# The mean of the heads' squares from unsplit squares in full-precision matmuls

## The chip, the cores and the metric

The kernel runs on one core of a Trainium2 chip. The metric is the device time of one execution in microseconds (us), the median of several runs. The engines are named as the profile names them: PE is TensorE (PEld its weight loads), DVE is VectorE, ACT is ScalarE, POOL is GpSimd, SP is the queue that issues the DMAs.

## What is computed

One layer of a hybrid decoder, for a prompt of 2048 tokens and a sample group of 8 x 4 tokens with the same weights. The change touches one term: the RMS norm of each head's output of the gated linear attention.

```
def _rmsnorm(x, g):
    xf = x.astype(jnp.float32)
    y = xf * lax.rsqrt(jnp.mean(xf * xf, axis=-1, keepdims=True) + EPS)
    return (y * g.astype(jnp.float32)).astype(x.dtype)
...
    h = _rmsnorm(x, lw['g_mix_pre'])
    proj = h @ lw['w_in']
    q, k, v, r, glr, u, vs = jnp.split(proj, SPLIT_POINTS, axis=-1)
...
    o, S_new = _gla(qh, kh, vh, gh, S0.astype(jnp.float32))
    o = _rmsnorm(o, lw['g_gla_out']).reshape(n, l, GLA_WIDTH).astype(x.dtype) * jax.nn.silu(r)
...
    mix = jnp.concatenate([o, s_out], axis=-1) @ lw['w_out']
    x = x + _rmsnorm(mix, lw['g_mix_post'])
```

There are 4 heads of 128 values each; the mean of the squares goes over a head's 128 values. After the mixer come a gated feed-forward part with a causal convolution and a gated per-layer embedding.

## The kernel before

It runs in five stages one after the other: the input projection, the mixer (`phase_mix`), the up projection with the convolution, the down projection, and the embedding. Large products are made in a rounded 32-bit type (F32R): each operand is split into a rounded copy and the rest that the rounding left, and three products (copy by copy, copy by rest, rest by copy) are summed.

The mixer walks over 16 tiles of 128 tokens in one hand-written order per engine, unrolled, as a loop of passes t = 0 to 19. Pass t works on several tiles at once: it makes scores, state and outputs of tile t (`turn_keys`, `make_scores`, `mix_positions`, `make_kv`, `within_chunk`, `from_state`), prepares the gates of tile t+1 (`gate_logits`, `soft_logs`, `exps`, `v_norm`), finishes the heads of tile t-1, and projects tile t-2 with the output weights (`project`, 48 matmuls of 512 columns in four groups). Tile 16 is the sample group, whose mixer work is done in passes 0 and 1. Every engine runs its own queue in order; semaphores join them. Each `within_chunk` (lines 809 to 819) of pass t overwrites the banks `o_acc`, so TensorE waits there for `gla_outs`, which VectorE raises in `finish_gla` of tile t-1 (line 1343).

The mean of a tile's squares takes these steps:
- ScalarE, `head_squares` (lines 992 to 999): the head outputs lie in two PSUM banks, `o_acc[0]` and `o_acc[1]`, 256 columns each. It squares each bank into `square` (line 997) and, from the bank again, into the rounded tile `square_h` (line 999). Behind it in ScalarE's queue come `copy_keys` (line 1006) and `soft_logs` (lines 1016 to 1023).
- GpSimd, `split_squares` (line 1151): `square_l` is `square` less `square_h`, in one instruction. Ahead of it in the queue is `row_powers` (lines 75 and 77), behind it `open_mixed` (line 1185) and `v_scale`.
- TensorE, `average_squares` (line 789): `m.average`, a 128 x 128 matrix of 1/128, times `square_h` and times `square_l`, summed in the other half of the bank. Two banks and two parts make four matmuls of 256 columns per tile. They stand in the middle of `project` of tile t-2, between its first and second group.
- ScalarE, `inverse_norm` (lines 1043 and 1047): logarithm and exponential give the inverse root; then `exps` of tile t+1 (line 1035) follow in its queue.
- VectorE, `finish_gla` (lines 1343 and 1352), far down its queue: it begins each pass with `scale_rows` (line 1374), which waits for `row_powers`, and has `mask` (1310), `v_stats`, `add_bias` (1336), the decays (1265 to 1279) and `v_norm` (1300) ahead of `finish_gla`.

The sample group has a mean of its own (line 898), which already multiplies the unsplit squares by `m.average` cast to F32.

Of the kernel before, what the change touches and what calls it, by code (L numbers as in the profile page):

```python
# [4 lines left out]
F32 = mybir.dt.float32  # L5
F32R = mybir.dt.float32r
I32 = mybir.dt.int32
ALU = mybir.AluOpType
ACT = mybir.ActivationFunctionType


P = 128
# [393 lines left out]
def phase_semaphores(nc, ctx, tag):  # L406


    held = []

    def clear():
        nc.clear_and_free_semaphores(held)
        nc.all_engine_barrier()
    ctx.callback(clear)

    def sem(name):
        held.append(nc.alloc_semaphore(name=f"{tag}_{name}"))
        return held[-1]
    return sem
# [96 lines left out]
def phase_mix(nc, a, pt_scratch, v_scratch, vs_scratch, residual, store, state_out, sample_state_out, vn_out,  # L516
# [4 lines left out]
    with ctx:  # L521
        sb = lambda n, s, d=F32: ctx.enter_context(nc.sbuf_tensor(f"mix_{n}", s, d))
        sem = phase_semaphores(nc, ctx, "mix")
        two = lambda n, s, d=F32: [sb(f"{n}{i}", s, d) for i in range(2)]
        m = MixerConsts(nc, ctx)
# [9 lines left out]
        with ExitStack() as placed:  # L535
# [17 lines left out]
        scores = sb("scores", [P, 2, 2, C])  # L553
        k_tok = sb("k_tok", [P, 2, P])
        state = two("state", [P, 2, DV])
        square, square_h, square_l = sb("square", [P, 2, 2 * P]), sb("square_h", [P, 2, 2 * P], F32R), \
            sb("square_l", [P, 2, 2 * P], F32R)
        inv = sb("inv", [P, 2, 2 * P])
        mixed = two("mixed", [P, 2 * H, P])

# [3 lines left out]
        ks_acc, o_acc = [bank("ks0"), bank("ks1")], [bank("o0"), bank("o1")]  # L564
# [10 lines left out]
        stat, v_power, v_normed, v_gained = (sem(n) for n in ("stat", "v_power", "v_normed", "v_gained"))  # L575
        scored, masked, k_turned, k_copied = (sem(n) for n in ("scored", "masked", "k_turned", "k_copied"))
        kv_made, states, outputs, crossed_made = sem("kv_made"), sem("states"), sem("outputs"), sem("crossed_made")
        squared, square_split, averaged, inverse = (sem(n) for n in ("squared", "square_split", "averaged", "inverse"))
        spatials, gla_outs, biased, sgu_outs = (sem(n) for n in ("spatials", "gla_outs", "biased", "sgu_outs"))
        state_stored = sem("state_stored")  # L580
        high, split, summed = sem("high"), sem("split"), sem("summed")
# [27 lines left out]
        def mixes(t):  # L609
            return 0 <= t < NT  # L610

        def projects(o):
            return 0 <= o <= NT
# [119 lines left out]
        def _(pe):  # L733
# [49 lines left out]
                last.then_inc(spatials, 1)  # L783

            def average_squares(t):
                pe.wait_ge(square_split, t + 1)
                for f in range(2):
                    for p, part_ in enumerate((square_h, square_l)):
                        last = nc.tensor.matmul(o_acc[f][:, 2 * P:4 * P], m.average[:, :], part_[:, f, :],
                                                start=(p == 0), stop=(p == 1))  # L790
                last.then_inc(averaged, 1)

            def make_kv(t):
# [127 lines left out]
            for h in range(HS):  # L921
                last = nc.tensor.transpose(m_acc[:, h * P:(h + 1) * P], spatial_raw[:, h, :], ident[:, :])
# [7 lines left out]
            for t in range(LAST):  # L930
# [12 lines left out]
                if mixes(t - 1):  # L943
                    average_squares(t - 1)
# [33 lines left out]
        def _(act):  # L978
# [12 lines left out]
            def head_squares(t):  # L991
                act.wait_ge(outputs, t * 2 + 2)
                if t >= 1:

                    act.wait_ge(averaged, t)
                for f in range(2):
                    nc.scalar.activation(square[:, f, :], o_acc[f][:, 0:2 * P], ACT.Square).then_inc(squared, 1)
                for f in range(2):
                    nc.scalar.activation(square_h[:, f, :], o_acc[f][:, 0:2 * P], ACT.Square).then_inc(squared, 1)

            def copy_keys(t):
                act.wait_ge(k_turned, t + 1)
# [103 lines left out]
            for t in range(LAST + 1):  # L1106
                if projects(t - 3):
                    row_squares(t - 3, 1)
                if mixes(t - 1):
                    head_squares(t - 1)  # L1110
                if mixes(t):
                    copy_keys(t)
                if mixes(t + 1):
                    soft_logs(t + 1)
                if t == 0:
                    sample_keys()
                if mixes(t - 1):
                    inverse_norm(t - 1)
                if mixes(t + 1):
                    exps(t + 1)  # L1120
                if t == 1:
                    sample_squares()
                    sample_inverse()
                if t < 2:
                    for k in range(4 * t, 4 * t + 4):
                        round_w(k)
                if projects(t - 1):
                    rounds(t - 1)
                if projects(t - 2):
                    row_squares(t - 2, 0)  # L1130

        @block.gpsimd
        def _(pool):
            def row_powers(o):
                s, rows = o % 2, out_rows(o)
                pool.wait_ge(row_squared, o * 2 + 2)
                if o >= 2:

                    pool.wait_ge(finished, (o - 1) * 2)
                rstd_ops(nc, pool, rstd[rows, s:s + 1], [part[rows, s, 0:1], part[rows, s, 1:2]],  # L1140
                         mean[rows, s:s + 1], consts[rows, :], powers, o * 3)

            def add_rest(o):
                s, rows = o % 2, out_rows(o)
                pool.wait_ge(res_in[s], o // 2 * 16 + 16)
                pool.wait_ge(finished, o * 2 + 2)
                nc.gpsimd.tensor_tensor(y[s][rows, :], y[s][rows, :], res[s][rows, :], ALU.add).then_inc(added, 1)

            def split_squares(t):
                pool.wait_ge(squared, t * 4 + 4)  # L1150
                nc.gpsimd.tensor_tensor(square_l[:, :, :], square[:, :, :], square_h[:, :, :].bitcast(F32),
                                        ALU.subtract).then_inc(square_split, 1)

            def v_scale(t):
                pool.wait_ge(stat, t * 8 + 8)
                nc.gpsimd.tensor_tensor(v_var[:, :], mv[:, :, 1:2].rearrange("p h a -> p (h a)"),
                                        consts[:, 0:1].to_broadcast([P, HS]), ALU.add).then_inc(v_power, 1)
                pool.wait_ge(v_power, t * 2 + 1)
                nc.gpsimd.tensor_tensor(v_rstd[:, :], v_var[:, :], consts[:, 1:2].to_broadcast([P, HS]), ALU.pow)\
                    .then_inc(v_power, 1)  # L1160

            def make_keys(t):
                s = t % 2
                if t >= 2:

                    pool.wait_ge(outputs, t * 2 - 2)
                for i, (out_, e) in enumerate(((k_in[s], e_k), (k_end[s], e_end))):
                    pool.wait_ge(factors, t * 4 + (i + 1))
                    nc.gpsimd.tensor_tensor(out_[:, :, :], qk[s][:, 2:4, :],
                                            e[:, :].rearrange("p (q t) -> p q t", q=2), ALU.mult).then_inc(keys, 1)  # L1170

            def v_tail(t):
                s = t % 2
                pool.wait_ge(v_normed, t * 4 + 4)
                if t == 0:
                    pool.wait_ge(loaded, 64)
                nc.gpsimd.tensor_tensor(vn[s][:, :], vn[s][:, :], m.ln_gain[:, :], ALU.mult).then_inc(v_gained, 1)
                pool.wait_ge(v_gained, t * 2 + 1)
                nc.gpsimd.tensor_tensor(vn[s][:, :], vn[s][:, :], m.ln_bias[:, :], ALU.add).then_inc(v_gained, 1)

            def open_mixed(t):
                s = t % 2
                pool.wait_ge(b_in[s], t // 2 * 32 + 32)
                pool.wait_ge(biased, t + 1)
                nc.gpsimd.tensor_tensor(mixed[s][:, H:2 * H, :], mixed[s][:, H:2 * H, :], ru[s][:, H:2 * H, :],
                                        ALU.mult).then_inc(sgu_outs, 1)
# [47 lines left out]
            for t in range(LAST + 1):  # L1234
                if projects(t - 3):
                    row_powers(t - 3)
                if mixes(t - 1):
                    split_squares(t - 1)
                if mixes(t):
                    open_mixed(t)  # L1240
                if mixes(t + 1):
                    v_scale(t + 1)
                if projects(t - 3):
                    add_rest(t - 3)
                if mixes(t + 1):
                    make_keys(t + 1)
                    v_tail(t + 1)
# [1187 lines left out]
def build(nc, a, outs):  # L2435
# [15 lines left out]
    with ctx:  # L2451
# [19 lines left out]
        with nc.sbuf_tensor("xh", [P, KC, T], F32R) as xh, nc.sbuf_tensor("xl", [P, KC, T], F32R) as xl:  # L2471
            phase_in(nc, x_tiles, xh, xl, a["w_in"][0], gains[:, 0, :], pt, v_s, vs_s, ident, consts)

        x1_of = lambda t: x1[token_rows(t), :]
        ffn = ctx.enter_context(nc.sbuf_tensor("ffn_features", [P, 2 * FC, 20], F32))
        phase_mix(nc, a, pt, v_s, vs_s, x_tiles, x1_of, outs[2][0, 0], outs[3][0], outs[6][0].rearrange("b t n -> (b t) n"),
                  [a["state_ffn_conv"][0].rearrange("b c n -> (b c) n"), a["w_conv"][0], a["b_conv"]], ffn, ident, consts)

# [51 lines left out]
```

## Time and profile before

| | us |
|---|---|
| median of 3 runs | 2875.97 (2875.3 to 2876.09) |
| the profiled execution | 2875.3 |
| its span, first to last instruction | 2873.6 |
| PE busy | 2660.5 (93%) |
| PE weight loads busy | 2398.4 (83%) |
| DVE busy | 1066.8 (37%) |
| ACT busy | 881.5 (31%) |
| POOL busy | 539.1 (19%) |
| mean granted TensorE clock | 0.951 |

All times of the trace are microseconds from the span's start. The mixer takes about 550 to 1009 us of it. Matmuls are pipelined, so the duration recorded of one is longer than the time from one to the next; the latter tells the price. A granted clock of 1.00 is 2.4 GHz, one of 0.50 is 1.2 GHz.

### The profile page before, as it was taken

How to read it: one execution, taken by the hardware profiler on the slowest of the kernel's cores; microseconds unless marked ns; L12 is line 12 of the kernel's file. 1: busy time of each engine (PE TensorE's matmuls, PEld its weight loads, DVE VectorE, ACT ScalarE, POOL GpSimd, SP SyncE). 2: the span in 40 equal slices, each digit the busy share in tenths (PEclk: the TensorE clock that was granted, in tenths of full speed). 3: DMA queues.
4: the chain of work that ended last, by engine and by line, in shares of the span. 5: the costliest groups of instructions: out<-in, count | busy, mean ns of one | idle time of the engine just before them, and what ended most of it. 6: DMA issues, size and time to landing. Idle time of an engine off the chain costs nothing. (4 is left out here: it accounts for less than half of the span.)

```text
span 2873.6 us, 36961 instructions
## 1 busy us (share of the span) xinstructions
PE 2660.5 (93%) x13748; PEld 2398.4 (83%) x13748; DVE 1066.8 (37%) x1635; ACT 881.5 (31%) x1781; POOL 539.1 (19%) x642
## 2 busy tenths in 40 slices
PE   7999999658888869999999999999799999996998
PEld 5789999556666669999999999999678888885887
DVE  4200000257666264444444444444422242324332
ACT  3311111123333263333333333333321142214332
POOL 2100000135544231111111111111000013221222
PEclk9999999759888989999999999999899999998999
DMA  4212221523333141111111111112454476643221
GB/s 147 91 63 67 70 67 62 136 78 113 102 100 93 59 150 53 42 53 38 50 50 42 56 38 50 41 47 73 120 143 111 119 219 192 192 133 123 83 79 44
DMA packets 270523, 257.54 MB, mean 90 GB/s; under 512 B 15830, under 2 KB 232422, under 8 KB 270406
## 3 DMA queue, kind: packets, MB, share of 16 engines
q1 hardware_dynamic: 270444, 256.51, 28.9%
q8 instruction: 47, 0.77, 0.1%
q14 instruction: 32, 0.26, 0.0%
HBM read 179.20 MB, written 77.26 MB: 89 GB/s over the span
## 5 line engine op out<-in xcount | busy, mean ns | idle before, releaser
L1857 PE MATMUL up_acc<-xh,up_wh 128*128 128x416 f32 x1760 | 619.6, 352 | 0.0
L1857 PE MATMUL up_acc<-xl,up_wh 128*128 128x416 f32 x1760 | 616.5, 350 | 0.0
L1857 PE MATMUL up_acc<-xh,up_wl 128*128 128x416 f32 x1760 | 616.1, 350 | 0.0
L1784 DVE SCALAR_TENSOR_TENSOR up_conv<-up_up,ffn_features,up_conv 128x416 f32<-128x416 f32 (+1 forms) x440 | 284.1, 646 | 570.4 <-ACT up_conv L1701 558.2
L1857 PEld LDWEIGHTS up_acc<-xh,up_wl 128*128 128x128 f32 x1760 | 330.1, 188 | 4.2
L1857 PEld LDWEIGHTS up_acc<-xl,up_wh 128*128 128x128 f32 x1760 | 330.8, 188 | 2.8
L1857 PEld LDWEIGHTS up_acc<-xh,up_wh 128*128 128x128 f32 x1760 | 329.9, 187 | 2.9
L2161 PE MATMUL down_acc<-down_wh,down_sh 128*128 128x512 f32 x748 | 293.3, 392 | 23.6 <-DVE down_sl L2092 23.6
L1695 ACT ACTIVATE up_up<-up_acc 128x416 f32<-128x416 f32 (+1 forms) x220 | 113.2, 515 | 606.3 <-PE up_acc L1857 606.3
L2161 PE MATMUL down_acc<-down_wl,down_sh 128*128 128x512 f32 x748 | 292.6, 391 | 0.0
L2161 PE MATMUL down_acc<-down_wh,down_sl 128*128 128x512 f32 x748 | 292.3, 391 | 0.0
L2161 PEld LDWEIGHTS down_acc<-down_wh,down_sh 128*128 128x128 f32 x748 | 141.4, 189 | 53.8 <-DVE down_sl L2092 24.6
L2092 DVE TENSOR_TENSOR down_sl<-down_raw,down_sh 128x2816 fp32r<-128x2816 f32 x34 | 110.9, 3262 | 192.9 <-ACT down_sh L2048 187.7
L1631 POOL COPY tail<-up_up 128x2 f32 (+1 forms) x44 | 22.6, 515 | 821.8 <-ACT up_conv L1701 821.8
L2161 PEld LDWEIGHTS down_acc<-down_wl,down_sh 128*128 128x128 f32 x748 | 141.4, 189 | 29.5
L2161 PEld LDWEIGHTS down_acc<-down_wh,down_sl 128*128 128x128 f32 x748 | 141.4, 189 | 29.5
L232 DVE TENSOR_TENSOR in_wl<-in_raw,in_wh 128x1024 fp32r<-128x1024 f32 x19 | 32.2, 1705 | 337.2 <-ACT in_wh L280 337.2
L1701 ACT ACTIVATE up_conv<-up_acc,ffn_features 128x416 f32<-128x416 f32 x220 | 154.8, 704 | 0.0
L287 ACT ACTIVATE in_outs<-in_acc 128x416 f32<-128x416 f32 (+2 forms) x86 | 47.2, 549 | 339.4 <-PE in_acc L393 194.2
L393 PE MATMUL in_acc<-xh,in_wh 128*128 128x416 f32 x416 | 146.2, 351 | 0.0
L393 PE MATMUL in_acc<-xl,in_wh 128*128 128x416 f32 x416 | 145.7, 350 | 0.0
L393 PE MATMUL in_acc<-xh,in_wl 128*128 128x416 f32 x416 | 145.4, 350 | 0.0
(271 smaller groups left out, 4311.9 us busy)
## 6 DMA issues: line engine op xcount, KB each, us to landing
down_raw<-hidden SPq DMA_DIRECT2D x34, 1408.0 KB, 7.6
hidden<-up_conv SPq DMA_DIRECT2D x110, 208.0 KB, 1.9
up_raw<-in_w_up SPq DMA_DIRECT2D x44, 512.0 KB, 3.9
proj_features<-in_outs SPq DMA_DIRECT2D x65, 208.0 KB, 1.9
down_ahead<-in_w_down SPq DMA_DIRECT2D x40, 256.0 KB, 5.3
in_raw<-in_w_in SPq DMA_DIRECT2D x19, 512.0 KB, 4.2
ple_x<-x SPq DMA_DIRECT2D x17, 512.0 KB, 4.3
in_x<-in_x_prompt SPq DMA_DIRECT2D x16, 512.0 KB, 3.6
```

What stands on the lines that cost most here:

```text
L232: nc.vector.tensor_tensor(wl[:, slot[n]], raw(n)[:, :, :], wh[:, slot[n]].bitcast(F32), ALU.subtract).then_inc(ready, 1)
L287: nc.scalar.activation(out[bank][rows, 0:width], acc[rows, 0:width], func)\
L393: last = nc.tensor.matmul(acc[bank][:, 0:TB], w[:, s, k, :], x[:, k, b * TB:(b + 1) * TB], start=(k == 0 and p == 0), stop=(k == KC - 1 an ...
L1631: nc.gpsimd.tensor_copy(tail[:, at, 0:2].rearrange("p a c -> p (a c)"), up[NBLK - 1][:, LAST:LAST + 2])
L1695: nc.scalar.activation(up[b][:, 2:2 + prompt], a[:, 0:prompt], ACT.Copy)
L1701: nc.scalar.activation(conv[b][:, :], a[:, 0:TB], ACT.Identity, scale=taps[:, at, 2:3].rearrange("p a c -> p (a c)"), bias=bias[:, at]).th ...
L1784: last = nc.vector.scalar_tensor_tensor(out=out, in0=x(c), in1=out, scalar=taps[:, at, c:c + 1].rearrange("p a c -> p (a c)"), op0=ALU.mul ...
L1857: last = nc.tensor.matmul(acc[b][:, 0:TB], w[kind][:, k, :], x[:, k, b * TB:(b + 1) * TB], start=(k == 0 and p == 0), stop=(k == KC - 1 an ...
L2092: nc.vector.tensor_tensor(sl[s][:, :, :], raw[s][:, :, :], sh[s][:, :, :].bitcast(F32), ALU.subtract).then_inc(split, 1)
L2161: last = nc.tensor.matmul(acc[s][:, :], x[s][:, k, :], ww[:, k, :], start=(k == 0 and p == 0), stop=(k == FC - 1 and p == 2))
```

## The change

`head_squares` keeps only the two squares into `square`. The tiles `square_h` and `square_l`, the GpSimd step `split_squares` and its semaphore go. `average_squares` waits for the two squares of its tile and makes one matmul per bank, 256 columns, of `m.average` cast to F32 and `square`, both in full 32-bit precision.

```
-        square, square_h, square_l = sb("square", [P, 2, 2 * P]), sb("square_h", [P, 2, 2 * P], F32R), \
-            sb("square_l", [P, 2, 2 * P], F32R)
+        square = sb("square", [P, 2, 2 * P])
...
-        squared, square_split, averaged, inverse = (sem(n) for n in ("squared", "square_split", "averaged", "inverse"))
+        squared, averaged, inverse = sem("squared"), sem("averaged"), sem("inverse")
...
             def average_squares(t):
-                pe.wait_ge(square_split, t + 1)
+                pe.wait_ge(squared, t * 2 + 2)
                 for f in range(2):
-                    for p, part_ in enumerate((square_h, square_l)):
-                        last = nc.tensor.matmul(o_acc[f][:, 2 * P:4 * P], m.average[:, :], part_[:, f, :],
-                                                start=(p == 0), stop=(p == 1))
+                    last = nc.tensor.matmul(o_acc[f][:, 2 * P:4 * P], m.average[:, :].bitcast(F32), square[:, f, :],
+                                            start=True, stop=True)
                 last.then_inc(averaged, 1)
...
                 for f in range(2):
                     nc.scalar.activation(square[:, f, :], o_acc[f][:, 0:2 * P], ACT.Square).then_inc(squared, 1)
-                for f in range(2):
-                    nc.scalar.activation(square_h[:, f, :], o_acc[f][:, 0:2 * P], ACT.Square).then_inc(squared, 1)
...
-            def split_squares(t):
-                pool.wait_ge(squared, t * 4 + 4)
-                nc.gpsimd.tensor_tensor(square_l[:, :, :], square[:, :, :], square_h[:, :, :].bitcast(F32),
-                                        ALU.subtract).then_inc(square_split, 1)
-
...
-                if mixes(t - 1):
-                    split_squares(t - 1)
                 if mixes(t):
                     open_mixed(t)
```

## Rows read from the trace of the kernel before

**Rows 1.** Busy by window: us; PE, PEld, DVE, ACT, POOL (x instructions); clock, DMA share, GB/s.
```profile
640.00:945.00 305.00, 259.23 (x1702) 204.81 (x1698) 207.83 (x416) 107.75 (x286) 152.66 (x156) 0.86 0.33 99
945.00:1010.00 65.00, 51.95 (x248) 41.14 (x248) 14.39 (x27) 11.76 (x29) 17.92 (x20) 0.94 0.15 53
```
**Rows 2.** Waits, 640 to 945 us: total us, times, longest us.
```profile
PE mix_o_acc L816 <- DVE mix_mixed L1343: 45.5, 12, 3.8
```
**Rows 3.** Timeline of PE, pass 12: start, duration, instruction [idle before it and who ended it].
```profile
872.52 1.16 PE L781 MATMUL mix_m_acc<-mc_spatial,mix_vn 128*128 128x128 f32 x8
873.44 0.48 PE L846 MATMUL mix_out_acc<-mix_wh,mix_sh 128*128 128x512 f32 x1
...
876.28 0.28 PE L789 MATMUL mix_o_acc<-mix_square_h,mc_average 128*128 128x256 f32 x1
...
876.74 0.40 PE L846 MATMUL mix_out_acc<-mix_wh,mix_sh 128*128 128x512 f32 x1
...
879.61 0.67 PE L803 MATMUL mix_ks_acc<-mix_v,mix_k_tok 64*64 64x128 f32 x16
884.07 1.12 PE L816 MATMUL mix_o_acc<-mix_scores,mix_v 64*128 64x64 f32 x8 [3.79 <-DVE mix_mixed L1343]
```
**Rows 4.** Timeline of ACT, pass 12.
```profile
871.79 0.67 ACT L999 ACTIVATE mix_square_h<-mix_o_acc 128x256 fp32r<-128x256 f32 x2
872.32 0.41 ACT L1006 ACTIVATE mix_k_tok<-mix_zt_acc 128x256 f32<-128x256 f32 x1
...
877.81 0.63 ACT L1047 ACTIVATE mix_inv<-mix_inv 128x512 f32<-128x512 f32 x1
878.83 0.42 ACT L1035 ACTIVATE mix_e_k<-mix_from_mid 128x256 f32<-128x256 f32 x1 [0.38 <-DVE mix_to_end L1279]
```
**Rows 5.** Timeline of POOL, pass 12.
```profile
872.53 1.28 POOL L1151 TENSOR_TENSOR mix_square_l<-mix_square,mix_square_h 128x512 fp32r<-128x512 f32 x1
875.85 1.60 POOL L1185 TENSOR_TENSOR mix_mixed<-mix_mixed,mix_ru 128x512 f32<-128x512 f32 x1 [2.04 <-DVE mix_mixed L1336]
```
**Rows 6.** Timeline of DVE, pass 12 and (977.28) pass 17.
```profile
872.53 1.41 DVE L1374 SCALAR_TENSOR_TENSOR mix_y<-mix_out_acc,mix_rstd,mix_gain_rows 128x512 f32<-128x512 f32 x2 [6.41 <-POOL mix_rstd L77]
...
883.27 0.74 DVE L1343 TENSOR_TENSOR mix_mixed<-mix_o_acc,mix_inv 128x256 f32<-128x256 f32 x2
...
977.28 1.41 DVE L1374 SCALAR_TENSOR_TENSOR mix_y<-mix_out_acc,mix_rstd,mix_gain_rows 128x512 f32<-128x512 f32 x2 [4.42 <-POOL mix_rstd L77]
```
**Rows 7.** Timelines of PE and ACT, passes 1 and 2.
```profile
612.34 0.58 PE L789 MATMUL mix_o_acc<-mix_square_h,mc_average 128*128 128x256 f32 x1
...
613.60 0.84 ACT L1043 ACTIVATE mix_inv<-mix_o_acc,consts 128x256 f32<-128x256 f32 x2 [14.52 <-PE mix_o_acc L789]
...
636.70 1.11 PE L826 MATMUL mix_o_acc<-mix_q_state,mix_state 64*128 64x64 f32 x8 [2.17 <-DVE mix_state L1326]
```
**Rows 8.** Busy by window, as in rows 1, behind four of PE's stalls.
```profile
693.54:699.04 5.50, 5.50 (x25) 4.61 (x26) 4.82 (x8) 1.63 (x3) 1.95 (x2) 0.50 0.65 195
...
860.15:866.25 6.10, 6.10 (x26) 5.11 (x27) 5.29 (x9) 1.63 (x3) 1.96 (x2) 0.50 0.67 208
...
962.29:965.25 2.96, 2.96 (x7) 2.38 (x8) 0.51 (x1) 0.00 (x0) 2.67 (x2) 0.50 0.00 0
...
993.75:1004.80 11.05, 11.05 (x48) 8.90 (x48) 0.51 (x1) 0.68 (x2) 2.40 (x1) 1.00 0.12 47
```
**Rows 9.** Timeline of PE, its stalls in passes 16 and 18.
```profile
962.29 0.77 PE L846 MATMUL mix_out_acc<-mix_wh,mix_sh 128*128 128x512 f32 x1 [2.24 <-DVE mix_y L1374]
...
993.75 0.47 PE L846 MATMUL mix_out_acc<-mix_wh,mix_sh 128*128 128x512 f32 x1 [2.82 <-DVE mix_y L1374]
```
**Rows 10.** Timeline of PE, the ends of three holes.
```profile
670.91 0.66 PE L816 MATMUL mix_o_acc<-mix_scores,mix_v 64*128 64x64 f32 x8 [3.80 <-DVE mix_mixed L1343]
...
693.54 1.12 PE L816 MATMUL mix_o_acc<-mix_scores,mix_v 64*128 64x64 f32 x8 [3.79 <-DVE mix_mixed L1343]
...
860.15 1.12 PE L816 MATMUL mix_o_acc<-mix_scores,mix_v 64*128 64x64 f32 x8 [3.79 <-DVE mix_mixed L1343]
```

## What I predict

> **What bounds the kernel now.** I read the busy times by stage first, then the waits, then one pass of the mixer loop engine by engine. The change touches only the mixer. In its steady part TensorE is busy 259 of 305 us and its granted clock averages 0.86 [rows 1]: it is neither full nor always fast. The waits name one hole: before the matmuls of line 816 TensorE stands still 12 times, 45.5 us in all, until VectorE has written `mixed` at line 1343 [rows 2]. That is once in each of the passes t = 3 to 14.
>
> Pass 12 shows how the loop closes. TensorE's last work before the hole starts at 879.61; the hole, 3.79 us, ends at 884.07 [rows 3]. Line 1343 doesn't wait for the squares' mean: the inverse is complete at 877.81 + 0.63 = 878.44 [rows 4], and VectorE reaches line 1343 only at 883.27 [rows 6]. What holds VectorE back is its own queue. It opens with `scale_rows` at 872.53, which waited 6.41 us for GpSimd's reciprocal root [rows 6], which goes back over ScalarE's `row_squares` to TensorE's last projection. So the loop runs TensorE's projection, ScalarE's row squares, GpSimd's root, VectorE's queue, TensorE again. The mean of the squares is beside this loop, with 883.27 - 878.44 = 4.8 us to spare.
>
> **Removed on ScalarE: two Square activations per tile.** They stand ahead of `copy_keys` and take 871.79 to 872.32, 0.53 us [rows 4], in all 16 x 0.53 = 8.5 us. `copy_keys` and the logarithms behind it could move up by that much at most, but what they feed, the decays on VectorE, stands in VectorE's queue behind `scale_rows`, which their absence doesn't release. On the path: 0. If that cover were gone, 0.53 us in each of 14 passes, 7.5 us.
>
> **Removed on GpSimd: `split_squares`,** 1.28 us per tile, 20.5 us in all. In pass 12 GpSimd then stands idle for 2.04 us until VectorE's line 1336 [rows 5], so its queue gains nothing. The subtraction runs exactly beside the two `scale_rows` instructions, which are on the path. If it slowed them, its removal would pay. The pair takes 1.41 us beside it (872.53), and 1.41 us in pass 17, where there is no subtraction (977.28) [rows 6]. On the path: 0.
>
> **Moved wait.** `average_squares` now waits for the two squares, issued before 871.79, where it waited for GpSimd until 872.53 + 1.28 = 873.81 [rows 4, 5]. TensorE reaches it at 876.28 without idle [rows 3], so nothing is queued behind a new wait: 0.
>
> **Changed on TensorE: four rounded products of 256 columns become two full-precision ones.** The four take 876.28 to 876.74, 0.46 us, 0.115 each [rows 3]. No row shows a full-precision product of 256 columns. The nearest is line 781 at 128: its four products are eight recorded matmuls, so one product is two of them, and they take 872.52 to 873.44, again 0.115 each [rows 3]. If the moving columns set that figure, 256 of them need 0.23, and a tile's four matmuls 0.92 us, 0.46 more than now. If the weight load sets it, which is 128 columns wide in both lines, a tile needs 4 x 0.115 = 0.46 us, 0.00 more. Line 803 decides: it has 64 weight columns and 128 moving ones and runs four at once. Its 16 matmuls take 0.67 us [rows 3]; less some 0.28 for one alone, that is 0.13 us between fours, no less than line 781's. Half the weight width saved nothing, so I take 0.46. For something unseen I keep twice the price, 1.84 us (+1.38), as the upper end, and 0.00 as the lower.
>
> The Trainium skill bears on this choice: "FP8 and Floating Point Precision", section TensorE Precision Notes, says that true FP32 makes four passes through the array. That is the first of the two readings; by the weight-load reading the sum would lose this term.
>
> **Where the 0.46 us falls.** In the 12 passes with the hole it only shortens the hole, from 3.79 to 3.33 us. The inverse ends at about 878.9 instead of 878.44, and ScalarE's exponentials, which start at 878.83 now because VectorE's decays are late [rows 4], move by some 0.1; what they feed on GpSimd comes behind 2 us of other work. So 12 x 0.
>
> Four tiles have no hole behind them.
> - Tile 0 (pass 1), at 612.34. The matmul is recorded at 0.58 us against 0.28 in pass 12, so the clock is at half, and ScalarE waited for the mean 14.52 us [rows 3, 7]. From there ScalarE, VectorE's queue and the sample matmuls lead without a gap to 636.70 [rows 7]. Cost at half clock: 2 x 0.46 = 0.9 us.
> - Tile 1 (pass 2): TensorE runs through to its projection: +0.46.
> - Tiles 14 and 15 (passes 15 and 16): TensorE is continuous up to its stalls, one of them before 962.29 [rows 9]: +0.46 each.
>
> Raw delay: 0.9 + 3 x 0.46 = 2.3 us. Not all of it lasts. Behind each hole the granted clock is 0.50, the lower of its two levels, 1.2 GHz: for 5.50 us in pass 4 and for 6.10 us in pass 11 [rows 8], though the work is the same. The period grows from 22.63 us (670.91 to 693.54) to 23.92 us (860.15 to 884.07) [rows 3, 10]. I read this as a loop that settles: a pass that starts later against the clock's return spends less time at half clock and gives part of the delay back. A delay brought in by tiles 0 and 1 should have died out by pass 14, and I count it 0 (end of the range 0.9 + 0.46 = 1.4). Left are tiles 14 and 15, 0.9 us.
>
> **Forecast.** The profiled execution's span is 2873.6 us, 2875.3 with what lies around it, 0.7 below the median. Against its own time the sum is 2876.2; on the median, 2875.97 + 0.9 = **2876.9 us**. What moves this by more than its own size is the clock at the mixer's end. A stall of 2.24 us before 962.29 is followed by 2.96 us at half clock, while one of 2.82 us before 993.75 costs none [rows 8, 9]. Shifting these stalls by 0.5 to 0.9 us may swap one for the other, 2.96 / 2 = 1.5 us either way for each, and the next stage begins at a clock that has to rise too.
>
> **Rivals.**
> - *The shorter hole keeps the clock up (faster).* "TensorE: Matmul & The Clock Gate" in the Trainium skill, section Why this matters for your kernels, asks for no long idle gaps between bursts, since the clock then falls; by that rule a shorter hole may be a gain. From rows: 6.10 us at half clock on the path are worth 3.05 us, times 11 about 33 us, hence 2843 us. Against it: a stall of only 2.24 us lost the clock [rows 8, 9], and the hole stays at 3.33. For it: one of 2.82 us kept it. Chance 0.04.
> - *The removed work was on the path after all (faster).* ScalarE's 7.5 us, hence 2869.4 us with the 0.9. Against it: the readings above [rows 4 to 6]. Chance 0.03.
> - *The full-precision product costs twice my price (slower).* At +1.38 us the 12 holes of 3.79 still cover it. Tile 0 at half clock costs 2.8, tiles 1, 14 and 15 1.4 each, 7 us if nothing is given back, hence 2883 us. It decides from +1.15 a tile (5 x 1.15 = 5.75). For it: no row at 256 columns. Against it: lines 781 and 803. Chance 0.06.
> - *The product isn't made in full precision* (two rounded products): 0.23 us saved in each of two tiles, 2875.5 us. Against it: no row; it would need the cast in the diff to be without effect. Chance 0.02.
>
> **How the numbers follow.** Forecast 0.85. A measurement of this kernel can tell about 0.2%, 5.75 us, from no change. Faster 0.04 + 0.03 less what of them stays small: 0.06. Slower 0.06. Within 0.2%: 0.88. The range is the forecast with three clock swaps of 1.5 us either way, and the 1.4 us of tiles 0 and 1 on the slow side, less what is unlikely to come together: 2872 to 2881.5 us.
>
> **What would show it.** In the changed profile: no GpSimd work between the root and line 1185, and 3.3 us idle before the latter; four recorded matmuls a tile at the mean, 0.23 us apart at full clock; the stall before line 816 still 12 times, near 3.3 us, with late periods of 23.9 us and the clock at 0.50 behind each. I would be wrong if the half clock is missing behind the holes, if the `scale_rows` pair falls under 1.41 us, or if TensorE waits at the mean.

## The result and the profile after

The changed kernel takes 2880.87 us in the median of 20 runs (2875.56 to 2882.47), the kernel before 2875.76 us in the median of its 20. The ratio is 1.0015 with a 95% interval of 1.0008 to 1.0022: 4.3 us slower, between 2.3 and 6.3 (the medians are 5.1 us apart). That is within 0.2%, inside the range of 2872 to 2881.5 us by 0.6 us, and 4 us above the forecast of 2876.9.

The profiled execution of the changed kernel has a span of 2877.2 us, 2879.04 with what lies around it. Its page counts 48 instructions less and, on TensorE, the same number:

```profile
span 2877.2 us, 36913 instructions
PE 2669.9 (93%) x13748; PEld 2405.7 (84%) x13748; DVE 1065.4 (37%) x1635; ACT 873.5 (30%) x1749; POOL 518.6 (18%) x626
```

ScalarE lost 8.0 us and GpSimd 20.5 us of work, as the change says; TensorE gained 9.4. Lines after 560 are numbered a few lower: line 789 is now 787, 816 is 814, 846 is 844, 1043 to 1047 are 1039 to 1043, 1343 is 1332, 1374 is 1363. The timeline of TensorE in pass 12, to be laid beside [rows 3]:

```profile
877.02 1.02 PE L787 MATMUL mix_o_acc<-mix_square,mc_average 128*128 128x256 f32 x4
880.75 0.67 PE L801 MATMUL mix_ks_acc<-mix_v,mix_k_tok 64*64 64x128 f32 x16
884.80 1.12 PE L814 MATMUL mix_o_acc<-mix_scores,mix_v 64*128 64x64 f32 x8 [3.39 <-DVE mix_mixed L1332]
```

The tile's two products are four recorded matmuls. From their start to the keys' products it is 3.73 us, where it was 3.33: 0.40 us more, and the hole is 0.40 us shorter, 3.39 for 3.79. The three other engines in the same pass, beside [rows 4 to 6]:

```profile
878.96 0.63 ACT L1043 ACTIVATE mix_inv<-mix_inv 128x512 f32<-128x512 f32 x1
879.55 0.42 ACT L1031 ACTIVATE mix_e_k<-mix_from_mid 128x256 f32<-128x256 f32 x1
...
876.59 1.58 POOL L1176 TENSOR_TENSOR mix_mixed<-mix_mixed,mix_ru 128x512 f32<-128x512 f32 x1 [3.36 <-DVE mix_mixed L1325]
...
873.27 1.41 DVE L1363 SCALAR_TENSOR_TENSOR mix_y<-mix_out_acc,mix_rstd,mix_gain_rows 128x512 f32<-128x512 f32 x2 [6.39 <-POOL mix_rstd L77]
...
884.01 0.74 DVE L1332 TENSOR_TENSOR mix_mixed<-mix_o_acc,mix_inv 128x256 f32<-128x256 f32 x2
```

`scale_rows` takes 1.41 us without the subtraction beside it, as with it. GpSimd waits 3.36 us for VectorE's line 1325 where it waited 2.04: its saving went into its own idle time. The inverse ends at 879.59, 4.4 us ahead of line 1332. So the loop is closed as before, and the wait list for 640 to 945 us shows it over all its passes:

```profile
PE mix_o_acc L814 <- DVE mix_mixed L1332: 40.7, 12, 3.4
```

12 holes, 40.7 us for 45.5 [rows 2], 0.40 less in each. The windows (columns as in [rows 1]) give the clock behind two of the holes and behind the three stalls at the mixer's end:

```profile
693.40:699.80 6.40, 6.40 (x27) 5.32 (x28) 5.29 (x9) 1.63 (x3) 1.92 (x2) 0.50 0.72 211
...
884.80:891.00 6.20, 6.20 (x26) 5.21 (x27) 5.22 (x9) 1.63 (x3) 1.96 (x2) 0.50 0.61 202
963.43:966.80 3.37, 3.37 (x15) 2.80 (x16) 0.52 (x1) 0.00 (x0) 2.38 (x1) 1.00 0.00 0
978.34:983.00 4.66, 4.66 (x14) 3.67 (x15) 0.84 (x2) 0.00 (x0) 2.42 (x1) 0.65 0.16 65
993.91:996.70 2.79, 2.79 (x7) 2.21 (x8) 0.51 (x1) 0.00 (x0) 2.13 (x1) 0.50 0.03 6
```

Behind the hole of pass 12 the clock is at half for 6.2 us, and behind that of pass 4 for 6.4 us; before, it was 6.1 us in pass 11 and 5.5 us in pass 4 [rows 8]. At the end two stalls have changed places: the one before 963.43 (before: 962.29) no longer costs the clock, the one before 993.91 (993.75) now does [rows 8, 9]. From the first matmul of line 814 in pass 15 (953.00; before 951.86) to the mixer's last matmul it takes 53.0 us, for 52.7 before.

### The profile page after: what moved, and what is told of

The parts are those of the page before. It is cut to its first block and busy times, and to the rows that moved or that the text cites. A ratio compares the mean times of both kernels' runs of the same rounds, so it can differ in the third digit from the quotient of the medians.

```text
span 2877.2 us, 36913 instructions
## 1 busy us (share of the span) xinstructions
PE 2669.9 (93%) x13748; PEld 2405.7 (84%) x13748; DVE 1065.4 (37%) x1635; ACT 873.5 (30%) x1749; POOL 518.6 (18%) x626
```

## The experiments

All comparisons are with the kernel before, which ran beside each; a ratio is turned into microseconds with 2876. Four to eleven runs of each edited kernel stand behind a median.

**Which tiles pay.** e1 puts the full-precision products into the twelve tiles with a hole behind them, e2 into the four without. ScalarE's and GpSimd's work stays in both. This is e1's edit; e2's condition is `not 2 <= t < NT - 2`.

```
             def average_squares(t):
                 pe.wait_ge(square_split, t + 1)
                 for f in range(2):
+                    if 2 <= t < NT - 2:
+                        last = nc.tensor.matmul(o_acc[f][:, 2 * P:4 * P], m.average[:, :].bitcast(F32), square[:, f, :],
+                                                start=True, stop=True)
+                        continue
```

> Only tiles 2 to 13, whose mean has the 3.8 us hole behind it, take the full-precision products (12 x 0.40 us more on TensorE, from the 0.215 us spacing of the changed kernel's trace); ScalarE's and GpSimd's work stays in all 16 tiles. Theory A, the hole covers it: 0 us against the kernel before, within 1 us; the holes shrink from 3.79 to 3.4 us and the clock still falls behind each. Rival B, the shorter hole changes where the clock comes back and costs on the average of many executions: +2 to +3 us.

Measured: 2875.89 us, ratio 1.0001 (0.9992 to 1.0011), +0.3 us. The interval reaches 3.2 us, so the times alone don't exclude rival B; that the covered tiles are free rests on the trace, where the loop keeps its period (908.39 to 932.27, 23.9 us). The holes are in its trace at 3.4 us, 40.6 us in all:

```profile
PE mix_o_acc L820 <- DVE mix_mixed L1347: 40.6, 12, 3.4
```

> Only tiles 0, 1, 14 and 15, with no hole behind their mean, take the full-precision products; the rest as before. Theory A as predicted, a delay of tiles 0 and 1 dies out in the loop: +0.8 us (tiles 14 and 15 alone). Theory A2, it dies out only against one position of the clock's return and counts in full over many executions: 0.85 + 3 x 0.40 = +2.05 us. Rival B (the cost is in the covered tiles): at most +0.8 us here.

Measured: 2878.56 us, ratio 1.0011 (1.0002 to 1.0020), +3.2 us (0.6 to 5.8). The twelve covered tiles cost nothing that can be measured, the four bare ones do. The interval of e2 holds 2.05 us and only just 0.8, so it leans to theory A2 without deciding it.

**The products against the removal.** e3 makes the new products in all tiles and keeps ScalarE's and GpSimd's work, which nobody needs any more but TensorE's wait. Its edit is e1's with a condition that is always true. e4 does the reverse: the removal alone, with the mean made from once-rounded squares. This is its edit against the changed kernel:

```
-        square = sb("square", [P, 2, 2 * P])
+        square = sb("square", [P, 2, 2 * P], F32R)
...
-                    last = nc.tensor.matmul(o_acc[f][:, 2 * P:4 * P], m.average[:, :].bitcast(F32), square[:, f, :],
+                    last = nc.tensor.matmul(o_acc[f][:, 2 * P:4 * P], m.average[:, :], square[:, f, :],
```

> Full-precision products in all 16 tiles, but ScalarE's second squares and GpSimd's subtraction still made, and TensorE still waiting for the latter. What it lacks against the changed kernel is the removal alone. If the removal is worth 0 (theory A): the same as the changed kernel, +4 to +5 us against before. If the removal itself costs (rival C: other timing on ScalarE, other addresses): +2 us only.

Measured: 2879.32 us, ratio 1.0012 (1.0003 to 1.0021), +3.5 us, between the two forecasts. The interval, 0.9 to 6.0 us, holds both.

> ScalarE's second squares and GpSimd's subtraction are gone, but the mean is made from squares rounded by ScalarE, in two rounded products per tile: the rest of the rounding is left out of the mean. Two matmuls of 0.115 us less per tile on TensorE. Theory A: -0.23 us in each of four bare tiles, double in tile 0, so -1.2 us. Rival C, the removal costs: +2 to +3 us. Rival D, the removed work was on the path: -7 us or more.

Measured: 2880.09 us, ratio 1.0016 (1.0007 to 1.0025), +4.6 us. This was the surprise: a kernel with less work on three engines is slower. Rival D, that the removed work was on the path, is out. Theory A's -1.2 us is out too. The parts also don't add: 3.5 and 4.6 us apart, 4.3 together.

**Is it the build?** e5 exchanges the places of the two tiles in memory and leaves every instruction as it was. e6 is the changed kernel with the freed memory kept as unused tiles. e11 repeats e4 in the same way, with later tiles at their old addresses.

```
+        unused = sb("square_h", [P, 2, 2 * P], F32R), sb("square_l", [P, 2, 2 * P], F32R)
```

> The kernel before with the two tiles square_h and square_l exchanged in the on-chip memory: the same instructions in the same order, only two addresses differ. It measures what a change without any effect on the work gives. Theory N (nothing but the work counts): 0, within 1 us. Rival H (each build has its own offset of some us, from where code and data lie): a difference of 2 us or more, in either direction.

Measured: 2876.30 us, ratio 1.0005 (0.9996 to 1.0014), no difference that can be told from none.

> The changed kernel with the 4 KB per partition that the removed tiles took kept as unused memory, so that all later tiles lie where they lay before. If the removal's cost in e4_removal_only (+4 us) comes from the moved addresses: at most +2 us against before. If it comes from the missing instructions or is chance: +4 to +5 us as the changed kernel.

Measured: 2879.12 us, ratio 1.0012 (1.0003 to 1.0021), +3.5 us. The interval reaches down to +0.9, so by itself it doesn't exclude the share of the addresses that was allowed for.

> e4_removal_only once more with later tiles at their old addresses: ScalarE's second squares and GpSimd's subtraction gone, the mean from squares rounded once, in two rounded products; the rest of the rounding is left out. If e4's +4 us is an effect of the removal itself: +4 us again. If it was the build's own offset or chance: between -2 and +2 us.

Measured: 2879.70 us, ratio 1.0014 (1.0004 to 1.0023), +4.0 us. With the addresses restored the removal costs the same again. Both intervals, on two builds, lie above 1 us: the addresses aren't it, and neither is chance.

**Where the removal's time lies.** The traces of e4 and e11 place most of it. Here are, for e4, the three stalls at the mixer's end (timeline of TensorE), and the windows behind them:

```profile
958.51 0.76 PE L844 MATMUL mix_out_acc<-mix_wh,mix_sh 128*128 128x512 f32 x1 [2.24 <-DVE mix_y L1363]
974.25 0.47 PE L844 MATMUL mix_out_acc<-mix_wh,mix_sh 128*128 128x512 f32 x1 [2.82 <-DVE mix_y L1363]
989.86 0.77 PE L844 MATMUL mix_out_acc<-mix_wh,mix_sh 128*128 128x512 f32 x1 [2.82 <-DVE mix_y L1363]
```

```profile
958.51:961.70 3.19, 3.19 (x8) 2.51 (x9) 0.52 (x1) 0.00 (x0) 2.37 (x1) 0.50 0.02 5
974.25:978.70 4.45, 4.45 (x13) 3.49 (x14) 0.84 (x2) 0.00 (x0) 2.42 (x1) 0.63 0.12 50
989.86:995.80 5.94, 5.94 (x14) 4.74 (x15) 0.51 (x1) 0.00 (x0) 2.37 (x1) 0.50 0.23 88
```

The stalls have the length they had before [rows 9], but every one now costs the clock, the last one for 5.94 us, where before it cost nothing behind that stall [rows 8]. e11 shows the same, in other absolute places:

```profile
962.43:965.60 3.17, 3.17 (x8) 2.49 (x9) 0.51 (x1) 0.00 (x0) 2.37 (x1) 0.50 0.03 5
...
993.77:999.60 5.83, 5.83 (x14) 4.57 (x15) 0.51 (x1) 0.00 (x0) 2.37 (x1) 0.50 0.24 92
```

From line 814's first matmul in pass 15 to the mixer's last matmul e4 takes 948.08 to 1003.45, 55.4 us, and e11 952.00 to 1007.35, 55.35 us. Before, it is 951.86 to 1004.52, 52.7 us. So 2.7 us come from there, though TensorE has 0.23 us less to do in it. The whole of the +4 us can be followed in e11's execution, which is at its median; its span is 4.1 us longer than before. It begins the stretch 0.14 us later, loses 2.7 us in it, 0.5 up to the next stage's first transpose and 0.8 behind that. e4's traced execution is the fastest of its eleven (2875.72 us): it begins the stretch 3.8 us earlier than before and still ends 0.2 us later.

That two executions agree to 0.02 us has a reason: the loop of passes 3 to 14 ends in one fixed place against the clock's return, so what follows meets the clock in the same way each time. From the end of pass 14's hole to the clock's return it is 6.1 to 6.2 us in all ten traces that have the holes. And the stretch takes 52.65 us in e1's trace and 52.67 in e5's, as before, and 52.97 in e2's and 53.02 in e6's, as in the changed kernel. e3 is the exception that tells most. Its TensorE does the same work as the changed kernel's, but with ScalarE's and GpSimd's work left in, the stretch takes 54.6 us, because its third stall costs 6.2 us at half clock for 2.8:

```profile
993.73:999.90 6.17, 6.17 (x15) 4.87 (x16) 0.51 (x1) 0.00 (x0) 2.37 (x1) 0.50 0.22 88
```

So e3 and e4 lose 1.6 and 2.3 us at the mixer's end that the whole change doesn't lose, and their costs needn't add up to its cost.

e12 takes the half clock away from this stretch and leaves the rest of e4 alone:

```
+                if t >= NT:
+                    for i in range(8):
+                        nc.tensor.matmul(m_acc[:, :], wh[:, i % KC, 0:P], wh[:, (i + 1) % KC, 0:512],
+                                         start=True, stop=True)
                 if projects(t - 2):
                     project(t - 2, 0, range(0, 4))
```

> e4_removal_only with eight extra rounded products of 512 columns ahead of each projection of passes 16, 17 and 18, whose result is never read; they take 1.85 us of the stalls of 2.24, 2.82 and 2.82 us there. The mean is again made from squares rounded once, the rest of the rounding left out. In e4's trace each of the three stalls was followed by half clock (3.2, 3.4 and 5.9 us or more from the next start), and from the last hole to the mixer's last matmul it took 55.4 us, where the kernel before took 52.7. Theory E (the removal's +4 us is half clock at the mixer's end): the clock stays at 1.00 behind the three stalls, that stretch takes 49 to 51 us, and the time is 4 to 6 us below e4, 2874 to 2876 us. Rival (the +4 us lie elsewhere or in the removal itself): the end gets shorter, but the time stays above 2877 us.

(The stretch that this text says begins at the last hole is the one above, from pass 15 on.) Measured: 2872.67 us, ratio 0.9987 (0.9978 to 0.9996), -3.7 us against before and -7.4 against e4's median. The last two of the three stalls and the end of the mixer in its trace:

```profile
974.68 0.47 PE L844 MATMUL mix_out_acc<-mix_wh,mix_sh 128*128 128x512 f32 x1 [1.02 <-DVE mix_y L1367]
988.64 0.47 PE L844 MATMUL mix_out_acc<-mix_wh,mix_sh 128*128 128x512 f32 x1 [1.01 <-DVE mix_y L1367]
```

All three starts are recorded at 0.47 us, the value at full clock, where e4 has 0.76 and 0.77. The stretch takes 949.96 to 999.40, 49.4 us, 5.9 less than e4. 24 matmuls whose result nobody reads make the kernel faster, and the removal's +4 us are gone with the half clock. Theory E holds, with a larger gain than it said. No run fills the stalls of the kernel before. Its own trace has 3.0 and 3.4 us of TensorE's work at half clock in the stretch, so without them I estimate 52.7 - 3.2 = 49.5 us for it, e12's figure within 0.1: the removal itself costs nothing there.

**The hole.** e7 fills the twelve holes of the changed kernel with unread products, e9 those of the kernel before.

```
                     make_kv(t)
+                    if 3 <= t < NT - 1:
+                        pe.wait_ge(biased, t + 1)
+                        for i in range(11):
+                            nc.tensor.matmul(m_acc[:, :], wh[:, i % KC, 0:P], wh[:, (i + 1) % KC, 0:512],
+                                             start=True, stop=True)
```

> The changed kernel with eleven extra rounded products of 512 columns in each of passes 3 to 14, issued between the keys' products and the wait for VectorE, into a bank that is free by then; their result is never read, the outputs stay complete. They take 11 x 0.23 = 2.55 us of the 3.39 us hole. Theory A (the half clock behind a hole is paid on the path): the clock stays at 1.00 through passes 3 to 14 and 6.1 us at half clock give back 3.05 us in each of 12 passes, -33 to -37 us, periods of 20.8 us. Rival (the loop is bound by something else, the half clock is free): 0 us. Rival (the extra reads slow the other engines): slower.

Measured: 2847.48 us, ratio 0.9909 (0.9893 to 0.9924), 33.4 us below the changed kernel's median (30.5 by the two ratios) and 26 below before. The window over its loop, and two passes' ends of the hole:

```profile
700.00:900.00 200.00, 193.43 (x1339) 150.84 (x1337) 152.63 (x306) 76.46 (x197) 101.09 (x106) 1.00 0.34 106
...
777.35 0.66 PE L814 MATMUL mix_o_acc<-mix_scores,mix_v 64*128 64x64 f32 x8 [0.73 <-DVE mix_mixed L1337]
...
798.47 0.66 PE L814 MATMUL mix_o_acc<-mix_scores,mix_v 64*128 64x64 f32 x8 [0.73 <-DVE mix_mixed L1337]
```

The clock stays at 1.00, the hole is 0.73 us, the period 21.12 us for 23.9. A period shorter by 2.8 us in twelve passes is 33 us.

> The kernel before (split squares) with the same eleven extra products in the hole of passes 3 to 14 as e7_hole_filled, never read. The hole is 3.79 us here, so 1.2 us of it stay open; the clock should still stay up. Theory A: -28 to -33 us against before, and 2 us below e7_hole_filled (the bare tiles' 2.05 us), 2844 to 2847 us. Rival (the half clock comes back through the wider hole): less than -20 us.

Measured: 2847.06 us, ratio 0.9899 (0.9884 to 0.9914). Its holes are 1.13 us and the period is 21.11. The 0.40 us of the products are all that differs in the hole. Against e7 it is 0.4 us lower by the medians and 2.9 by the ratios; 2 us between them were expected, and four runs of each can't tell.

**The move.** e8 and e10 put useful work into the hole instead, in the changed kernel and in the one before.

```
                 if mixes(t):
                     make_kv(t)
+                if projects(t - 2):
+                    project(t - 2, 1, range(0, 4))
+                if mixes(t):
                     if t >= 1:
 
                         pe.wait_ge(gla_outs, t * 4 - 2)
...
                     from_state(t, 0)
-                if projects(t - 2):
-                    project(t - 2, 1, range(0, 4))
                 if mixes(t):
```

> The changed kernel with one move in TensorE's order: the first half of the second projection (12 matmuls of 512 columns) goes ahead of the wait for VectorE instead of behind it. The hole shrinks from 3.39 to about 0.6 us, the clock stays up, and the 2.8 us of projection leave the loop TensorE, ScalarE, GpSimd, VectorE. Theory A: periods of 18 to 18.6 us for 23.9, -60 us or more in 12 passes. Rival (another wait closes the loop at once, VectorE's state update before the second from_state being the nearest): only the clock's share, -33 to -40 us.

Measured: 2816.05 us, ratio 0.9793 (0.9776 to 0.9810), -60 us against before, -65 against the changed kernel.

> The kernel before with the move of e8_reordered and split squares. TensorE has almost no hole left there, so nothing covers the full-precision products of the changed kernel any more, 12 x 0.40 us in the loop and 2.05 us outside it. Theory A (cover gone, the products cost): 5 to 7 us below e8_reordered, 2809 to 2811 us. Rival (the loop is closed by VectorE, which is as slow in both): equal to e8_reordered within 2.5 us. Rival (the removed work counts once the hole is gone): above e8_reordered.

Measured: 2812.54 us, ratio 0.9788 (0.9775 to 0.9802). Both beat both kernels. Between them lie 3.5 us by the medians and 1.4 by the ratios. With four and five runs that scatter by 4 us, this can't tell theory A's 5 to 7 us from none. The traces say more of the steady loop. Two rows each of e8 (first) and e10:

```profile
784.26 0.66 PE L814 MATMUL mix_o_acc<-mix_scores,mix_v 64*128 64x64 f32 x8
...
789.56 0.66 PE L824 MATMUL mix_o_acc<-mix_q_state,mix_state 64*128 64x64 f32 x8 [0.52 <-DVE mix_state L1316]
```

```profile
761.37 0.66 PE L816 MATMUL mix_o_acc<-mix_scores,mix_v 64*128 64x64 f32 x8 [0.33 <-DVE mix_mixed L1344]
...
766.66 0.66 PE L826 MATMUL mix_o_acc<-mix_q_state,mix_state 64*128 64x64 f32 x8 [0.49 <-DVE mix_state L1327]
```

In e10 the hole is 0.33 us and TensorE waits another 0.49 us for the state that VectorE advances. In e8 the 0.40 us of the products have filled the first hole, and the second wait is 0.52. VectorE's queue closes the loop in both, with a period of 18.3 us (747.63 to 765.95 in e8, 743.05 to 761.37 in e10). In the steady loop the cover had changed its place, not gone. But e8's loop isn't always steady. Behind waits of only 0.70 us (before 691.08) and 0.74 us (before 844.79) its clock fell to half:

```profile
846.80:850.10 3.30, 3.30 (x16) 3.01 (x13) 2.97 (x13) 1.84 (x6) 0.37 (x1) 0.50 0.45 127
```

Those two passes took 19.9 and 20.2 us for 18.3, and nothing like it stands in e10's loop. Whether the full-precision products bring that on isn't shown.

## Why the prediction was right and where it fell short

The time lies in the range, but the forecast of +0.9 us lies below the measured interval of 2.3 to 6.3. The range was wide for clock swaps of 1.5 us each, and in the changed kernel's trace these come out nearly even; that the time fell inside is in part luck.

- *The chain.* Right. The mean of the squares lies beside the loop; after the change the spare time is 4.4 us for the 4.8 read from [rows 4, 6].
- *The removed work on ScalarE and GpSimd: 0 on the path.* Right for the loop: `scale_rows` kept its 1.41 us, GpSimd's saving turned into idle time, and the loop's period is unchanged. But the kernel with the removal and cheaper products (e4, e11) is 4 us slower, 2.7 us of it at the mixer's end. The step that missed this is the one that priced each edit in its own pass only.
- *The moved wait: 0.* Right; TensorE reaches the mean without idle.
- *The price of the full-precision product.* Right in its reading, 15% high in size: 0.40 us more per tile at full clock for the predicted 0.46, and 0.85 at half clock for 0.9. The columns set it, not the weight load. "FP8 and Floating Point Precision" in the Trainium skill, section TensorE Precision Notes, gives four passes for true FP32. The trace agrees: a product takes 2 x 0.215 = 0.43 us, 3.7 times the rounded one's 0.115, though it is recorded as two matmuls and not as four.
- *Twelve tiles under the hole.* Right by e1's trace; its time, +0.3 us (-2.3 to +3.2), fits.
- *Tiles 0 and 1 counted at 0.* This is the step that failed, at least in its reason. The loop does settle: from pass 8 on its starts lie 0.71 to 0.76 us behind those of before (884.80 and 884.07). But it settles on the clock's return, and that stands elsewhere in each execution. In the changed kernel's profile the mean of tile 0 begins 2.43 us earlier than before (609.91 and 612.34), and the settled loop ends 0.75 us later. In e4's it begins 0.31 us earlier than in the changed kernel's (609.60), and the last hole ends 4.33 us earlier (928.26 and 932.59); the start and the cheaper products of tiles 0 and 1 make only 2.2 us of that by my estimate (0.31 + 1.28 + 0.63). The settling doesn't swallow a delay, it rounds it to the clock, up or down. If the clock's place varies freely between executions, an early delay costs its full size on the average. By that the sum is 0.85 + 3 x 0.40 = 2.05 us, not 0.9. e2 measures 0.6 to 5.8 us for it, which fits and doesn't prove it.
- *The clock swap at the mixer's end.* Right in the mechanism and in the place: the stall before 962.29 got its clock back and the one before 993.75 lost it, in the changed kernel's profile. It was taken as scatter on both sides. e4, e11 and e12 show that it isn't scatter: since the loop ends at a fixed place against the clock, each edit of some tenths of a microsecond sets it the same way each time (e6's trace repeats the changed kernel's pattern, e5's that of before). For the changed kernel it comes out nearly even (53.0 for 52.7 us); for the removal alone it is 2.7 us.
- *The rivals.* The shorter hole doesn't keep the clock up at 3.39 us; at 1.13 and 0.73 it does (e9, e7), and its value was sized rightly: 33 us forecast, 33.4 by the medians and 30.5 by the ratios. The doubled product price and the product that isn't full precision are out by the recorded 0.40 us.
- *The rule on idle gaps.* "TensorE: Matmul & The Clock Gate" in the Trainium skill, section Why this matters for your kernels, asks for no long idle gaps between bursts. The traces agree in direction. No length of a gap tells by itself: 2.24 us cost the clock in one kernel and not in the next, at the same place of the program [rows 8, 9], and in e8 the clock fell behind waits of 0.70 and 0.74 us.

What stays open: the sum with this correction is about 2.4 us, against a measured 4.3, whose interval begins at 2.3. It is 2.05, less 0.04 in the end stretch, and some 0.4 where the next stage begins: 18.2 us from the mixer's last matmul to its first transpose, for 17.9. (e1's trace has 18.2 there too, so that part may be scatter.) The other 2 us weren't placed. One profiled execution of each kernel can't place them, because single executions of the kernel before already lie between 2868 and 2879 us.

The times of all executions narrow it. The device time exceeds the span by 1.7 us in the mean of the kernel before (83 executions beside the experiments) and of each kernel that keeps the removed work, and by 1.9 to 2.0 us in the changed kernel and each with the removal. So 0.2 us lie outside the span; what takes them isn't shown. The mean granted clock is 0.9505 over the changed kernel's 20 executions and 0.9514 over those 83. I estimate from that 2 x 0.0009 x 2876 = 5 us more at half clock, worth at most 2.6 us where TensorE is on the path. Part of this is tile 0's delay or the end's, already counted. It could hold the rest, but no run shows where.

## What to carry to other kernels

Before adding up work saved or added beside a stall, look at the granted clock behind the stall: here each of twelve holes of 3.8 us cost 2.8 us more in half clock, seven times what the change moved. A loop that loses its clock once a pass may lock to it; then small edits inside vanish, and small edits behind it come out as the clock decides, with either sign. Unread matmuls in the holes were worth some 30 us. Moving independent work ahead of the wait is the better remedy: one moved group of 12 matmuls in each pass was worth 60 us. And one trace is one execution: compare its time with the median before reading a cause from it.

## What the runs showed of the hardware

- A full-precision product of 128 x 128 weights and 256 columns is two recorded matmuls, 0.215 us apart at 2.4 GHz and 0.427 at 1.2 GHz (2.07 us for four, with the tail); the rounded one is a single one of 0.115 us.
- Unread matmuls in a stall shorten the kernel: 132 of them in twelve holes gave 29 to 33 us (e9, e7), 24 of them in three stalls gave 7.4 (e12 against e4, 5.9 of it in the stretch with the stalls).
- A kernel that does less can be slower by a reproducible 4 us (e4, e11). 2.7 us of it come from where three stalls of unchanged length meet the clock, and all of it was gone when they were filled (e12).
- The clock fell to half behind a wait of 0.74 us in e8 and stayed up behind one of 2.82 us in the kernel before: the length of one stall doesn't decide it.
- An exchange of two tiles' addresses changed nothing that could be measured (1.0005, 0.9996 to 1.0014).
